# A batched 32x32 triangular inverse moved from VectorE to GpSimd in a two-block transformer kernel

## The reference: what is computed

```
strict = jnp.tril(jnp.einsum('bhcid,bhcjd->bhcij', kbeta, kc) * decay, -1)
rhs = jnp.concatenate([vc * betac[..., None], kbeta * jnp.exp(gc)[..., None]], axis=-1)
sol = lax.linalg.triangular_solve(strict, rhs, left_side=True, lower=True, unit_diagonal=True)
```

## Time and profile before

| what | value |
|---|---|
| time, median of 3 runs | 2338.57 us (2338.34 to 2343.1) |
| the profiled execution, its own time | 2338.74 us |
| its span in the trace | 2336.9 us |
| busy: TensorE / VectorE / ScalarE / GpSimd | 2155.0 / 1188.4 / 788.1 / 906.9 us |
| mean granted TensorE clock, share of full speed | 0.971 |

### The profile page before, as it was taken

How to read it: one execution, slowest core, us unless ns; L and a number is a source line. 1 busy time by engine, 2 the same in 40 slices (tenths; PEclk the granted TensorE clock), 3 DMA queues, 4 the chain that set the end, 5 groups by cost and what they waited for, 6 DMA issues and landing times. The chain is left out here.

```text
span 2336.9 us, 29185 instructions
## 1 busy us (share of the span) xinstructions
PE 2155.0 (92%) x10931; PEld 1813.2 (78%) x10931; DVE 1188.4 (51%) x1706; ACT 788.1 (34%) x1434; POOL 906.9 (39%) x611
## 2 busy tenths in 40 slices
PE   6999988778997899999999996988999999999997
PEld 5788877668775688888888875777887888888886
DVE  4443504866436735555555557678996154201232
ACT  4333225455224342222222224237775122000112
POOL 2222321332236766666666665230000333323334
PEclk9999999889999899999999998999999999999999
DMA  4121311020212111111111132310000111111131
GB/s 153 40 51 43 82 47 24 14 50 33 99 46 82 45 52 48 46 46 54 55 55 55 55 110 77 103 36 2 1 1 24 45 48 43 51 49 45 54 117 73
DMA packets 164188, 125.95 MB, mean 54 GB/s; under 512 B 25316, under 2 KB 144848, under 8 KB 163920
## 3 DMA queue, kind: packets, MB, share of 16 engines
q1 hardware_dynamic: 148576, 91.77, 13.4%
q10 hardware_dynamic: 15472, 32.31, 3.8%
HBM read 106.77 MB, written 17.30 MB: 53 GB/s over the span
## 5 line engine op out<-in xcount | busy, mean ns | idle before, releaser
L940 POOL TENSOR_SCALAR w_hi<-w_raw 128x1024 fp32r<-128x1024 f32 x113 | 130.8, 1157 | 988.3 <-issue 916.6
L1059 PE MATMUL gemm<-h_hi,w_hi 128*128 128x512 f32 x1072 | 423.3, 395 | 8.4 <-POOL h_lo L969 4.6
L1061 PE MATMUL gemm<-h_hi,w_lo 128*128 128x512 f32 x1072 | 418.5, 390 | 0.0
L1060 PE MATMUL gemm<-h_lo,w_hi 128*128 128x512 f32 x1072 | 418.4, 390 | 0.0
L943 POOL TENSOR_TENSOR w_lo<-w_raw,w_hi 128x1024 fp32r<-128x1024 f32 x113 | 283.9, 2513 | 9.4
L1059 PEld LDWEIGHTS gemm<-h_hi,w_hi 128*128 128x128 f32 x1072 | 202.3, 189 | 52.7 <-issue 8.0
L1061 PEld LDWEIGHTS gemm<-h_hi,w_lo 128*128 128x128 f32 x1072 | 202.0, 188 | 42.6
L1060 PEld LDWEIGHTS gemm<-h_lo,w_hi 128*128 128x128 f32 x1072 | 202.4, 189 | 40.6
L1871 DVE TENSOR_TENSOR acc<-acc,gemm 128x1024 f32<-128x1024 f32 x80 | 97.7, 1221 | 116.1 <-PE gemm L1080 115.9
L936 POOL TENSOR_TENSOR w_lo<-wsum,w_hi 128x512 fp32r<-128x512 f32 x100 | 136.9, 1369 | 28.4 <-ACT w_hi L1507 22.1
L1507 ACT ACTIVATE w_hi<-wsum 128x512 fp32r<-128x512 f32 x100 | 63.3, 633 | 200.3 <-POOL wsum L923 197.3
(11 more groups left out here) (413 smaller groups left out, 4408.9 us busy)
## 6 DMA issues: line engine op xcount, KB each, us to landing
w_raw<-in_w_in SPq DMA_DIRECT2D x60, 512.0 KB, 3.8
w_raw<-in_ffn_w_gate SPq DMA_DIRECT2D x22, 512.0 KB, 3.7
w_raw<-in_ffn_w_up SPq DMA_DIRECT2D x22, 512.0 KB, 4.2
w_raw<-in_ffn_w_down SPq DMA_DIRECT2D x22, 512.0 KB, 3.9
w_raw<-in_w_out SPq DMA_DIRECT2D x16, 512.0 KB, 3.7
x_spill<-x ACTq DMA_DIRECT2D x4, 2048.0 KB, 6.6
xin<-in_x SPq DMA_DIRECT2D x8, 512.0 KB, 6.5
x<-in_x ACTq DMA_DIRECT2D x1, 4096.0 KB, 15.8
```

The lines of the kernel that those rows point to most:

```text
L940: gp.tensor_scalar(hi[:], raw[key % 4][:], 1.0, 0.0, ALU.mult, ALU.add).then_inc(pool_hi, 1)
L1059: mm(o, hi[:, k, m], act[0][:, k, t], start=k == 0, stop=False)
L1060: mm(o, hi[:, k, m], act[1][:, k, t], start=False, stop=False)
L1061: last = mm(o, lo[:, k, m], act[0][:, k, t], start=False, stop=k == kt - 1)
```

## The change

The items `("inv", j)` are done by GpSimd and no longer by VectorE. The list of items is the same, the tiles, the arithmetic and the semaphores too.

```
@@ block.gpsimd, between the items "st" and "gx"
+                elif kind == "inv":
+                    if j == 0:
+                        pool.wait_ge(w_split, job_of[rec_weight - 3] + 1)
+                        step(gp.memset(Xb, 0.0))
+                        step(gp.memset(Xb.rearrange("p i n -> p (i n)")[:, 0:1024:33], 1.0))
+                        pool.wait_ge(a_in, 16)
+                    n, m = 31 - j, j + 1
+                    t = btmp[:, 0:n, 0:m]
+                    step(gp.tensor_tensor(t, AB[:, j, m:32].unsqueeze(2).to_broadcast([P, n, m]),
+                                         Xb[:, j, 0:m].unsqueeze(1).to_broadcast([P, n, m]), ALU.mult))
+                    step(gp.tensor_tensor(Xb[:, m:32, 0:m], Xb[:, m:32, 0:m], t, ALU.subtract))
+                    if j == 30:
+                        step(gp.tensor_copy(AB[:], Xb.rearrange("p i n -> p n i")), "inv_done")
@@ block.vector
-                elif kind == "inv":
...
-                        step(v.tensor_copy(AB[:], Xb.rearrange("p i n -> p n i")), "inv_done")
```

## The result

The changed kernel takes 2353.43 us (median of 4 runs, 2353.15 to 2353.69), the kernel before 2340.78 us beside it (median of 4, 2338.34 to 2343.10). The ratio is 1.0053 with a 95% interval of 1.0041 to 1.0065: slower by 12.65 us (the interval spans 9.6 to 15.2). The profiled execution took 2353.69 us with a span of 2351.9, 14.95 us more than the profiled one of before. That one took 2338.74 us, near the two shorter of the four executions of before (2338.34, 2338.57, 2342.99 and 2343.10); this is most of the difference between 12.65 and 14.95.

A forecast was written before the change was run, and what follows sets the result against it. VectorE was taken to bound the inverse's four rounds, GpSimd's ring after the change: 4 x 12.73 + 40.1 sets + 1.0 disturbance = 92.0 us against 75.69, so 2338.74 + 16.3 = 2355 us; range 2350 to 2366.

The forecast's parts named there:

- The ring: Four rounds with inverse steps: ScalarE's `ed`, GpSimd's gate, ScalarE's squares wait in turn; a round takes 12.73 us plus its set.
- the whole set stands inside the GpSimd ring: On GpSimd each set stands behind `xc` (L998), which needs `ed`, and before the next `st`, so idle time doesn't hide it.
- The sets: Four groups of inverse steps on GpSimd, with memsets and a copy: 9.1, 11.4, 11.2 and 8.4 us, 40.1 in all.
- the rival of dearer rows: In GpSimd's inverse steps, short rows cost half as much again per element: +26.6 us, 2365 us; chance 0.14.
- The disturbance: VectorE and GpSimd slow each other in the four rounds: GpSimd loses 0.25 us a round, 1.0 in all; VectorE's loss is hidden.
- `sn` hidden: ScalarE's eight scalings of `sn`, in the third of the four rounds, are hidden behind GpSimd's set and add nothing.
- Downstream: Transfer of the inverse's blocks to ScalarE's first `gx`: slack falls from 3.3 to 1.7 us, still hidden, costing nothing.
- all of it reaches the end: From 510 us on, no load or split can take up the shift, so the whole +16.3 us arrives at the end.
- The faster rival: The sets hide in GpSimd's idle time and rounds fall back to 13.22 us: -22.8 us, 2316 us; chance 0.03.

The follow-up runs named there:

- the run with every second set: Changed kernel with sets 1 and 3 left on GpSimd, sets 2 and 4 on VectorE as before, semaphores between the two: 2337.87 us, ratio 0.9989.

## Why the prediction was right

**The ring.** Right, and to a few hundredths of a us: 12.73 us plus the set gives three of four rounds. The step "the whole set stands inside the GpSimd ring" was tested from two sides: with the sets elsewhere on the same engine the rounds fall to 15 to 18 us (2326.34), and with ScalarE's link cut the first two fall to 14.64 and 13.70. One reading in the prediction is off in its words: 424.71 is where the four rounds begin and not the end of the first; the sum of 75.69 is right.

**The sets.** Foretold 9.1, 11.4, 11.2 and 8.4, measured 9.58, 12.07, 11.32 and 8.60: 41.57 against 40.1. The rates hold (617 and 727 ns for 256 elements against 0.61 and 0.73), and short rows cost nothing extra (243 ns for 31 elements against 0.18 us + 31 x 1.68 ns = 0.23 us). So the rival of dearer rows falls. The memset took 0.951 us (I took 1.0), the copy 1.938 (1.8). The estimate of 2.5 us for that copy from the Trainium skill, page "GPSIMD Engine Reference", section "Performance pitfalls for Q7 kernels", is too high for this read, whose step is 128 bytes. The ratio of 1.96 of the Trainium skill, page "GPSIMD Engine Reference", section "Elementwise — side-by-side cycle accounting", gave, in the prediction's estimate with a factor of two, 59 us for the sets, 17 more than they took.

**The disturbance.** Foretold 1.0 at 0.25 a round, measured about 1.3, and unevenly. Two steps were stretched inside the sets, the one of 175 elements above (0.89 us; its other occurrence, 498.61, took 0.56) and one in the second set (1.02, against 0.62 for one of its size): 0.7 us that the measured sets hold. In the third round L998 starts 0.28 us later behind `ed` than in the first, and L1003 takes 1.59 and not 1.26: together 0.61 of the 0.64 us by which that round is longer (why L998 started later I don't know). The four sets and the disturbance together were short by 1.1 us.

The larger part of the disturbance falls on VectorE. The prediction named only L2216 and "some tiny ones", and the tiny ones are stretched most:

```profile
504.77 1.81 DVE L2123 TENSOR_TENSOR amx<-amx,sinkb 128x4 f32<-128x4 f32 x1
```

The same instruction takes 0.16 us in every round of the kernel before. Here it ends at 506.58, with GpSimd's copy (504.62 + 1.94 = 506.56). Over the four rounds the means of L2216, L2123 and L2125, all with two inputs in SBUF, go from 692, 162 and 162 ns to 1068, 786 and 546: 5.5 us in twelve instructions. It costs nothing here, as foretold: ScalarE waits for none of these results in the four rounds.

**`sn` hidden.** Right in the changed kernel: the third round isn't longer for its eight scalings. It holds only as long as GpSimd's set covers them. With the sets out of the ring that round is the longest, 19.04 us, and without the item 13.78.

**Downstream.** Nothing waited for the blocks, and the transfer kept its distance to the gate, as said (0.39 us against 0.43; slack about 2.3 us against 1.7). But "all of it reaches the end" did not hold, by little: the rounds grew by 93.17 - 75.69 = 17.5 us, the first `gx` came 18.3 late, 2.6 came back up to the first scaling of the recurrence state, and 15.0 arrived. The foretold +16.3 was 1.2 us too small in the rounds and did not reckon with what comes back; the two errors partly cancel. The absolute figure flatters the forecast too: 2355 stands only 1.6 us above the 2353.43 measured, but it was built on 2338.74 us for the kernel before, which took 2340.78 beside the changed one. As a difference, +16.3 stands against 14.95 between the traces and against 12.65 between the medians, and lies just above the interval's 15.2. That is luck in the number; the mechanism doesn't rest on it.

**The faster rival.** Its number, 2316, was worked out from rounds of 13.22 us, which no kernel reached without more being changed: without any step it was 2322.49. The rounds around the inverse are longer for two reasons that the prediction's rival didn't price, a TensorE clock of 0.82 and `sn`. With the clock held up and `sn` moved, the sets spread over six idle times took 2316.32; that it meets the rival's number doesn't make the rival right, since the changed order gives no idle time to hide in.

## What to carry to other kernels

Before moving work to an engine with much idle time, find the two instructions between which it would stand, and ask if what ends the idle time comes before or after them. Here one place cost 31 us against no steps and the other, one instruction earlier in the same list, 4. Taking the work out of one ring makes the next term visible (an item, a clock, a late transfer), so a floor should be measured with the work left out and not taken from a quiet round elsewhere.

## What was not expected of the hardware

In the rounds in which TensorE waits, its mean granted clock was lower (0.82 to 0.83) although it was busy for 40.76 of 47 us, and this slows a ring that runs through TensorE: rounds of 15.1 to 15.5 us against 13.3 to 14.0 (14.8 in the first) with seven unread products added, and 8.4 us of the time. The round with `sn` is no part of this. In rounds that GpSimd sets, the same products brought nothing (2328.71 against 2326.34). In the changed kernel the granted clock was 0.71 in the second and third of the four rounds, and the rounds were as foretold, since the ring passes GpSimd and ScalarE.

VectorE and GpSimd slow each other, and a short instruction can pay for a long one: a VectorE operation on 128x4 took 1.81 us in place of 0.16 beside GpSimd's copy. In the run with every second set, four VectorE steps of 207 and 220 elements took 1.11 to 1.33 us each beside GpSimd's operations of 512 elements, where before steps of that size took 0.38 to 0.39.
